# Attention written as one unrolled pipeline of 128 tiles, with projections in pieces and the scaling of P on GpSimd

## What is computed

```
h = rmsnorm(x);  q, k, v = split(h @ w_in)
s = q @ k.T * scale + bias;  p = softmax(s);  o = p @ v        # per head
x = x + concat(o) @ w_out
h = rmsnorm(x);  x = x + (silu(h @ w_gate) * (h @ w_up)) @ w_down
```

## Time and profile before

| | us |
|---|---|
| three timed executions, median | 3236.41 |
| the profiled execution, its span | 3236.5 |
| PE busy, of that span | 2955.4 (91%) |
| DVE busy | 1586.8 (49%) |
| ACT busy | 1111.6 (34%) |
| POOL busy | 710.7 (22%) |

### The profile page before, as it was taken

The page is one execution under the profiler, slowest core; times in us unless marked ns, Lnnn a source line. Parts: engine busy times, 40 slices in busy tenths (PEclk is TensorE's granted clock), DMA queues, the critical chain, the costliest instruction groups (busy, mean ns, idle before and its releaser), DMA issues.

```text
span 3236.5 us, 42169 instructions
## 1 busy us (share of the span) xinstructions
PE 2955.4 (91%) x14200; PEld 2381.7 (74%) x14200; DVE 1586.8 (49%) x2457; ACT 1111.6 (34%) x1827; POOL 710.7 (22%) x450
## 2 busy tenths in 40 slices
PE   6888898888899999999987888888898999999997
PEld 2677776666678888888765777777775888888885
DVE  4755565565243233223348777777714332323235
ACT  2655555554110000000135777777702001000101
POOL 1111101103423223332310000000323323332331
PEclk8999999999899999999998999999999999999998
DMA  3111111113111111111121111111221111111111
GB/s 132 60 49 37 50 44 38 37 37 130 45 38 47 52 45 45 52 48 49 52 66 45 37 37 36 36 37 41 78 100 39 46 45 52 52 45 45 52 45 52
DMA packets 195091, 167.79 MB, mean 52 GB/s; under 512 B 35258, under 2 KB 181042, under 8 KB 194226
## 3 DMA queue, kind: packets, MB, share of 16 engines
q1 hardware_dynamic: 183370, 140.05, 14.2%
q10 hardware_dynamic: 11680, 27.24, 2.6%
HBM read 146.03 MB, written 21.23 MB: 52 GB/s over the span
## 4 chain that ended last, share of the span: by engine, by line
PE 76%; DVE 8%; ACT 7%; issue 7%; DMA 1%; ACTq 1%; DVEq 1%; POOL 0%; SPq 0%; POOLq 0%
PE psS L481 15%; PE psS L483 15%; PE psS L482 15%; PE psS L549 5%; PE psD L651 5%; PE psD L647 5%; PE psD L649 5%; PE psD L579 5%; PE psD L566 4%; ACT xT L795 2%; DVE psD L953 2%; DVE pt L1016 2%; DVE rstd L948 1%; DVE hT L960 1%; PE psD L502 1%
## 5 line engine op out<-in xcount | busy, mean ns | idle before, releaser
L481 PE MATMUL psS<-hT,W 128*128 128x512 f32 x2208 | 868.4, 393 | 48.1 <-DVE hT L960 21.7
L482 PE MATMUL psS<-hT,W 128*128 128x512 f32 x2208 | 862.7, 391 | 0.0
L483 PE MATMUL psS<-hT,W 128*128 128x512 f32 x2208 | 862.1, 390 | 0.0
L393 POOL CAST W<-stage 128x1024 fp32r<-128x1024 f32 (+1 forms) x185 | 193.1, 1044 | 1806.4 <-PE psS L483 1144.1
L481 PEld LDWEIGHTS psS<-hT,W 128*128 128x128 f32 x2208 | 416.3, 189 | 149.9 <-issue 23.8
L483 PEld LDWEIGHTS psS<-hT,W 128*128 128x128 f32 x2208 | 416.5, 189 | 87.3
L482 PEld LDWEIGHTS psS<-hT,W 128*128 128x128 f32 x2208 | 416.7, 189 | 85.4 <-issue 1.0
L395 POOL TENSOR_TENSOR W<-stage,W 128x1024 fp32r<-128x1024 f32 (+1 forms) x185 | 442.4, 2391 | 14.8
L1103 DVE TENSOR_TENSOR row<-psS,row 128x512 f32<-128x512 f32 x88 | 60.9, 692 | 739.9 <-PE psS L483 739.9
L566 PE MATMUL psD<-flip_t,xT 128*128 128x128 f32 x1856 | 272.2, 284 | 70.7 <-DVE pt L1016 57.2
L1016 DVE TENSOR_TENSOR pt<-psD,pt 128x512 fp32r<-128x512 f32 (+2 forms) x512 | 301.6, 629 | 44.0 <-ACT pt L784 41.9
(11 more groups left out here) (104 smaller groups left out, 2494.1 us busy)
## 6 DMA issues: line engine op xcount, KB each, us to landing
stage<-in_w_gate SPq DMA_DIRECT2D x44, 512.0 KB, 3.8
stage<-in_w_up SPq DMA_DIRECT2D x44, 512.0 KB, 3.8
stage<-in_w_down SPq DMA_DIRECT2D x44, 512.0 KB, 3.6
xT<-rel_c SPq DMA_DIRECT2D x16, 960.0 KB, 4.5
stage<-in_w_even SPq DMA_DIRECT2D x24, 512.0 KB, 5.6
park<-xT ACTq DMA_DIRECT2D x2, 4096.0 KB, 13.9
heads<-o_out ACTq DMA_DIRECT2D x128, 64.0 KB, 1.9
xT<-park ACTq DMA_DIRECT2D x4, 2048.0 KB, 11.1
```

The costliest lines, as they stand in the source:

```text
L481: pe.matmul(o, wop(0, k), rhs(0, k, h), start=n == 0, stop=False)
L482: pe.matmul(o, wop(0, k), rhs(1, k, h), start=False, stop=False)
L483: mm = pe.matmul(o, wop(1, k), rhs(0, k, h), start=False, stop=n == len(ks) - 1)
```

## The change

Both attention phases lose their hardware loops. Each is now one unrolled run of 128 tiles (`TILES`), A and B together and C by itself, with constants in the waits. The pipeline does not drain between pairs.

- The projections of the first pair are still done ahead. Those of each later pair are cut into **pieces** that PE runs at the end of the steps of the pair before. A and B: a half weight is two pieces of 12 matmuls, so 12 pieces in steps 5 to 16 (`filler_even`). C: eight pieces of 3 or 9 matmuls in steps 7, 8, 9, 11, 12, 13, 15 and 16 (`filler_c`). All pieces use one PSUM bank, `ps_p`, and each waits until the one before it has been evicted. The evictions are at the start of the next step on ACT, and behind the bias on DVE.
- The scaling of P is on POOL for all tiles (`normalise`), between halves of weight splits.
- In a step ACT now does eviction, exp of tile t, then the copies of tile t-2. DVE does bias of t, eviction, low parts of t-2, reciprocal of t. Before, the reciprocal was that of t-1 and ACT's copies stood ahead of the exp.
- The values have one PSUM bank instead of two, `PT` holds three tiles, `W` two weights, K and Q operands are in three slots.
- SP issues the stores of the heads; V is turned in steps 2 and 3 of its own pair. B's tables are built by DVE in steps 10 and 3. Projection splits of heads 0 to 3 go on POOL between the scalings of the last pair.

The core of the diff, with the rest of the renaming left out:

```diff
-            with pe.Fori(0, 4, 1) as it: ... product(...) ; turn_v ; attention(...)
+            for n in range(6):
+                even_product(0, n, 0)
+                even_product(0, n, 1)
+            for t in range(-1, TILES + 3):
...
+                    scores(0, t + 1, window_even, even_operands)
+                if 2 <= t < TILES + 2:
+                    turn_scores(0, t - 2, window_even)
+                if t >= 4 and t % 2 == 0:
+                    values(0, (t - 4) // 2, window_even)
+                if step in (2, 3) and 0 <= pair < PAIRS:
+                    turn_v(0, pair, step - 2)
+                if filler_even(t):
+                    even_product(*filler_even(t))
...
+            for t in range(TILES + 5):                                   # ACT
+                if t and filler_even(t - 1) and filler_even(t - 1)[2]:
+                    even_evict(*filler_even(t - 1)[0:2])
+                if step in (3, 4) and pair < PAIRS:
+                    keep_v_hi(0, pair, step - 3)
+                if t < TILES:
+                    exp_scores(0, t, window_even)
+                if 2 <= t < TILES + 2:
+                    keep_p_hi(0, t - 2, window_even)
+                if t >= 5 and t % 2 == 1:
+                    keep_o_lo(0, (t - 5) // 2)
...
+            for t in range(TILES + 5):                                   # DVE
+                    bias_scores(0, t, window_even, t < TILES // 2)
+                    even_evict(*filler_even(t - 1)[0:2])
+                    keep_v_lo(0, pair, step - 3)
+                    keep_p_lo(0, t - 2, window_even)
+                    reciprocals(0, t)
+                if t >= 5 and t % 2 == 1:
+                    sum_o(0, (t - 5) // 2)
...
-                            ve.tensor_scalar(s, s, r, None, ALU.mult).then_inc(S["nm0"], 1)
-                        sc.activation(s, s, ACT.Copy, scale=rden[:, 1:2]).then_inc(S["nm1"], 1)
+            def normalise(t0, t, window):                                # POOL
+                s = score(t)[:, 0:window(t)[1]]
+                pool.wait_ge(S["recip"], t0 + t + 1)
+                pool.tensor_scalar(s, s, rden[:, t % 4:t % 4 + 1], 1.0, ALU.mult, ALU.mult).then_inc(S["normed"], 1)
...
+                if kind == 1:                                            # C, rotary piece: DVE, then ACT r_hi, then DVE r_lo
+                    ve.scalar_tensor_tensor(other, o[HD:P, :], C_SCALE, ...)
+                    ve.scalar_tensor_tensor(rq, rq, C_SCALE, cos_t[0:HD, cols], ...)
+                    ve.tensor_tensor(rq, rq, other, ALU.add).then_inc(S["r_rot"], 1)
```

More of the change, by code:

```diff
@@ L457, in _ @@
             pool.wait_ge(S["sc"], at("attn_c", "sc", 0))
-            with pool.Fori(0, NC_PAIRS, 1) as it:
-                split("attn_c", 0, 0, ("sc", 4 - 20, 20), it, 1, dmas=8, buf=0, swap=swap_rotary)
-            pool.wait_ge(S["sc"], at("proj_1", "sc", 4 - 20))
+            for half in range(2):
+                latent_split(0, half)
+            for t in range(TILES):
+                pair, step = t // NSTEP, t % NSTEP
+                normalise(TILES, t, window_c)
+                if pair < PAIRS - 1 and step in (1, 3):
+                    latent_split(pair + 1, step // 2)
+                if pair == PAIRS - 1 and step in (8, 10, 12, 14):
+                    split_heads("proj_1", (step - 8) // 2)
             proj_weights("proj_1")
@@ new lines, in values @@
+            def values(t0, g, window):
+                k0, nk, _ = window(2 * g)
+                pe.wait_ge(S["p_lo"], 2 * t0 + 4 * g + 4)
+                if g:
+                    pe.wait_ge(S["o_sum"], t0 // 2 + g)
+                if g % 8 == 0:
+                    pe.wait_ge(S["v_lo"], (t0 + 2 * g) // 8 + 2)
+                a, b = 2 * g % 3, (2 * g + 1) % 3
+                units = slice(a, a + 2) if b == a + 1 else slice(a, None, -2)
+                n = 0
+                for j in range(nk // P):
+                    for s in range(2):
+                        mm = pe.matmul(blocks(ps_o[:, 0:256]), vv[:, k0 // P + j, g // 4 % 2, :],
+                                       PT[:, s, j, units, :], start=n == 0, stop=n == 2 * nk // P - 1)
+                        n += 1
+                mm.then_inc(S["pv"], 1)
@@ new lines, in keep_o_lo, with keep_v_row @@
+            def keep_o_lo(t0, g):
+                sc.wait_ge(S["pv"], t0 // 2 + g + 1)
+                if g:
+                    sc.wait_ge(S["o_sum"], t0 // 2 + g)
+                sc.activation(o_lo[:, :], ps_o[HD:P, 0:256], ACT.Copy).then_inc(S["o_lo"], 1)
+            def keep_v_row(t0, pair, h, bank):
+                n = t0 // 8 + 2 * pair + h
+                if pair:
+                    sc.wait_ge(S["v_turn"], n - 1)
+                sc.activation(row[:, h * HALF:(h + 1) * HALF], bank, ACT.Copy).then_inc(S["v_row"], 1)
@@ new lines, in _ @@
+            for n in range(8):
+                c_evict(0, n)
+            for t in range(TILES + 5):
+                pair, step = t // NSTEP, t % NSTEP
+                if t and filler_c(t - 1):
+                    c_evict(*filler_c(t - 1))
+                if step in (3, 4) and pair < PAIRS:
+                    keep_v_hi(TILES, pair, step - 3)
+                if t < TILES:
+                    exp_scores(TILES, t, window_c)
+                if 2 <= t < TILES + 2:
+                    keep_p_hi(TILES, t - 2, window_c)
+                if t >= 5 and t % 2 == 1:
+                    keep_o_lo(TILES, (t - 5) // 2)
@@ L924, in _ @@
+            gather_heads("proj_1", TILES)
             norm("norm_f1")
@@ new lines, in _ @@
+            for n in range(6):
+                c_evict(0, n)
+            for t in range(TILES + 5):
+                pair, step = t // NSTEP, t % NSTEP
+                if t < TILES:
+                    bias_scores(TILES, t, window_c, True)
+                if t and filler_c(t - 1) and filler_c(t - 1)[1] < 6:
+                    c_evict(*filler_c(t - 1))
+                if step in (3, 4) and pair < PAIRS:
+                    keep_v_lo(TILES, pair, step - 3)
+                if 2 <= t < TILES + 2:
+                    keep_p_lo(TILES, t - 2, window_c)
+                if t < TILES:
+                    reciprocals(TILES, t)
+                if t >= 5 and t % 2 == 1:
+                    sum_o(TILES, (t - 5) // 2)
```

896 lines of the change are left out of this document (479 added, 417 removed).

## The result

Four timed executions of the changed kernel gave 3287.25 to 3292.48 us, median 3288.86; four of the kernel before beside them 3236.42 in the median. The ratio is 1.016, with a 95% interval of 1.0145 to 1.0174. I had forecast 3214 and a range up to 3285, so the result lies outside the range and on the other side of zero. The profiled span is 3290.4 us.

A forecast was written before the change was run, and what follows sets the result against it. The prediction took a serial DVE and ACT chain to bound steps without a piece and all of C, and PE plus open evictions the others. 3236.5 less 27 (even phase) plus 5 (C) gave, rounded, 3214 us; range 3160 to 3285.

The forecast's parts named there:

- The chain: Attention steps without a piece: bias, exp, copies, low parts, reciprocal, next bias in series, 4.29 us, 4.63 in odd steps.
- A pairs: Even phase: PE's work plus open evictions in 12 steps, four steps without pieces; 87.0 us against 92.57, the last 85.7.
- B pairs: Even phase, smaller windows: pieces, PE's other work and 8.0 of open evictions, four steps without pieces; 75.4 us against 79.4.
- B's last pair: End of the even phase, no pieces: steps 5 to 15 and drain take 39.8 us.
- SP and the rest: Stores add 128 issues to SP, with slack; the projection after each phase starts as before; nothing for both.
- C: Second attention phase: 77.4 us a pair against 79.14, two rotary steps 3.0 longer each; whole phase 615.5 against 610.5, +5.
- The first bias: Start of the even phase: it can come 2 us earlier, as V's copy and turn no longer stand ahead.
- POOL's scaling: Scaling of P in attention steps: taken as 2.4 us, between a 1.05 cast and a 2.40 subtraction; hidden, free below 4.2.
- The tables: B's table additions on DVE: 16 waits for POOL of at most 1.8 us, some 10 more than the sum if half open.
- No chain (3075): Rival for attention steps: copies and exp overlap, so the busiest engine sets the step; 140 less, 3075; chance 0.10.
- Piece and chain in series (3305): Rival for A and B steps with pieces: a step costs 4.46 plus its piece, 2.72; 91 more, 3305; chance 0.20.
- The clock: Rival: idle PE falls to 1.2 GHz in the last B pair; costs about 5, 20 if it spreads, 3235; chance 0.05.

The follow-up runs named there:

- The filled gap: The changed kernel with 20 unused matmuls of 256 columns ahead of each piece that waits for K's low parts; 3277.09 us.
- the heads in halves: The changed kernel with POOL's splits of the first four head tiles in eight halves and their loads issued in step 2, not 6; 3284.71 us.
- the weights early: The changed kernel with the first two weights of the projection behind each attention phase loaded in step 10 of the last pair; 3276.52 us.
- The copies first: The changed kernel with ACT's copies ahead of the exp again and DVE's reciprocal, of tile t-1, ahead of the low parts; 3159.69 us.
- the bank, the loads and the heads were mended: The changed kernel with copies ahead of exp, old reciprocal order, pieces one step earlier, heads split in halves and first projection weights loaded early; 3092.99 us.
- a third cost 166: The changed kernel with DVE's bias of tile t+1 moved ahead of the eviction and low parts of step t; 3454.44 us.

## Why the prediction was wrong, point by point

- **The chain: right, in size too.** 4.29 and 4.63 were forecast for steps without a piece, 4.28 to 4.42 and 4.60 were measured. ACT idle before the exp and DVE idle before the low parts are as described. The extra 0.14 of many steps goes with PE: its transposes wait for the low parts of the tile before (L654, 53.4 us), and ACT's copies for the transposes (42.4 us).
- **A pairs: 87.0 forecast, 89.7 to 91.3 measured from step 5 to step 5; the last, into B, 85.7 forecast and 90.3 measured. Together 14 of 76.** PE's wait behind K was put at 2.2 and measured 2.49. V's eviction was covered, as I wrote, but the sum has no term for what comes behind it: the values and the second turn of V wait for V's low parts, 1.56 and 1.24 us in an A pair. The four steps by the chain should have been 2 x 4.29 + 2 x 4.63 = 17.8, not 17.4. The third pair has 1.6 of clock besides.
- **B pairs: 75.4 forecast, 82.2, 82.1 and 84.8 measured. This is 23 of 76, the largest miss but C's.** The waits behind K and Q were about right: 8.0 forecast, 3.15 and 1.09 twice each measured, 8.5. What failed is that a piece takes PE 2.72 wherever it stands: behind a wait of 3.15 it took 4.41. The filled gap gave 3.5 a pair back in the profiled execution. V's low parts, behind two table additions and a bias on DVE, cost a wait of 3.47 and one of 1.19 more.
- **B's last pair: 39.8 forecast from step 5, 46.7 measured.** "SP and the rest: nothing" failed. POOL's wait for the heads' load was queued ahead of the scalings: one step of 7.0 us, 3.4 with the heads in halves (and 3.7 in one run without that edit). The rest, 3, is the drain and small parts of other steps.
- **C: 615.5 forecast, 641.9 measured, 26 of the miss.** Rotary steps took 7.82, not 7.3: 7 in all. In four of seven pairs the step behind them was 6.9 to 7.0 in place of 4.74, with PE at a clock of 0.50 in the stretch shown above: 9. The transposes in many steps: 4. The drain took 16.4 in place of 10.5. Half of that is the last values at the low clock, 3.76 and 3.40 us in place of 2.15; the rest stays open:

```profile
2390.14 3.76 PE L671 MATMUL psD<-pt,vv 128*128 128x256 f32 x16
...
2396.90 3.40 PE L671 MATMUL psD<-pt,vv 128*128 128x256 f32 x16 [2.05 <-DVE o_out L1197]
```

- **"The projection after each phase starts as before": wrong, 12.** I had counted slack for each store but not that the load of the first weight was to stand behind the last of them on SP. The run with the weights early gave 12 back.
- **The first bias: 2 forecast, 8.9 measured**, the one miss in the good direction. The traces place it. PE's first projection matmul started 6.3 us earlier, at 69.02 in place of 75.28, and the rest, 2.6, is the term that I had. Of the 6.3, DVE's first scaling in the norm came 2.7 earlier. The other 3.5 go with its first three: before, they ran beside POOL's splits of 1024 columns and took 2.89, 1.53 and 2.13 us; after, they took 0.76 each, for POOL splits these weights in halves of 512 columns and was done at 52.7. No run tried it apart. The first two of them, before and after:

```profile
60.88 4.33 DVE L953 SCALAR_TENSOR_TENSOR psD<-xT,gain,rstd 128x512 f32<-128x512 f32 x2
...
58.14 1.42 DVE L1134 SCALAR_TENSOR_TENSOR psD<-xT,gain,rstd 128x512 f32<-128x512 f32 x2
```

- **POOL's scaling: right.** The mean of a full tile was 1.13 us in the groups, near the cast, as the bound that I took the nearer one by; doubled it cost nothing. The Trainium skill ("GPSIMD Engine Reference", Engine selection) has one-input operations roughly at line rate; by that rule, the trace agrees.
- **The tables.** I left 10 us for them outside the sum (half of 16 waits of 1.8 would have been 14). All additions together were worth 5 to 11, of which 6 were in the sum, and there was no wait for POOL among them. The Trainium skill ("SBUF — State Buffer", Who interferes with whom) says that a DVE instruction with two SBUF inputs contends with a GpSimd instruction that reads SBUF, and that issue order decides who blocks; I had carried over only the half in which DVE waits. The trace agrees with neither half as a rule for this pair: beside all eight tables it was POOL's scaling that was stretched, 0.91 to between 2.58 and 3.00 us, while the additions took 1.07, and in four of the eight POOL had started first, by some 0.14 us, as in the lines above. The measurement decides: the cost fell on the engine that had slack.
- **The rivals.** No chain (3075) was refuted by the trace. The copies first took the chain out and gave 3160, and 3093 once the bank, the loads and the heads were mended: the rival's price was near what the chain and its neighbours cost. Piece and chain in series (3305) is the nearest in time, but not what happened: A's steps with Q and V stayed near PE's work, and only K's were in series. The clock I priced at 5 for the idle steps of B's last pair and 20 if it spread to the free steps; it was a cost behind the long waits for K and for the rotary pieces, in steps with a piece.

In one sentence: the mechanism was right and its sum was a forecast of a gain of 22, less than the terms at the edges (clock behind waits, V's low parts, the queues of SP and POOL at the end of a phase), each of which I had put at nothing.

## What to carry to other kernels

When two engines hand a tile back and forth, put each engine's work in the order in which its inputs become ready, and check for each wait what is queued behind it; here two swaps of program order were worth 129 us and a third cost 166. Work for a shared buffer goes where the longest other work stands ahead of its next use: moving pieces by one step was worth 47. A wait of PE of some 3 us cost half as much again in the matmuls behind it, so price both, and look at the queues (stores before loads, waits before scalings) at the end of each phase, where there is no cover.

## What the runs showed of the hardware

- TensorE's granted clock in a stretch of 4 us behind a wait of some 3 us was 0.50 to 0.61, and a piece of 12 matmuls took 4.41 us in place of 2.72. With matmuls of no use in the wait it took 2.82, and the kernel was 12 us faster. Shorter waits were followed by a fall in some pairs and not in others of the same code: three of eight waits of 2.49 in A, three of seven waits of 1.62 in C.
- POOL's `tensor_scalar` with a scalar for each partition, 128x1024 in float32, takes 1.13 us, near the cast of 1.05.
- Beside DVE additions with two inputs in SBUF, POOL's 0.91 us scaling of 768 columns took 2.99, whichever of the two had started first; behind the even phase three of DVE's subtractions of 1024 columns took 6.49 (the shortest single one 1.21) while POOL's took 3.20 in place of 2.40; and in the norm ahead of the first pair it was DVE that lost, up to 2.89 for 0.76. Either side can lose.
